# Making the keys of the third mixer inside the stage of the gated recurrence

## The reference, cut to what matters

```python
# rwkv7_branch
a = jax.nn.sigmoid(a0 + pa @ a_up)
g = jax.nn.sigmoid(pg) @ g_up
kk = k * k_k
k = k * (1.0 + (a - 1.0) * k_a)
kk = kk / jnp.maximum(jnp.sqrt(jnp.sum(kk * kk, axis=-1, keepdims=True)), 1e-12)   # per head of 64
y = rwkv7_recurrence(r, decay, k, v, -kk, kk * a)
bonus = jnp.sum(r * k * r_k, axis=-1, keepdims=True) * v
# rglru_branch
xb = causal_dwconv(px, conv_w, conv_b)
gate_a = jax.nn.sigmoid(blockwise(xb, w_ga) + b_ga)
gate_x = jax.nn.sigmoid(blockwise(xb, w_gx) + b_gx)
log_a = LRU_C * gate_a * jax.nn.log_sigmoid(lam)
mult = jnp.sqrt(-jnp.expm1(2.0 * log_a))
u = xb * gate_x * mult
_, h = lax.associative_scan(_lin_combine, (jnp.exp(log_a), u), axis=1)
return h * jax.nn.gelu(py)
```

## Time and profile before

| | |
|---|---|
| median of 3 runs | 2880.39 us (2879.45 to 2884.05) |
| the profiled execution: its time | 2888.27 us |
| its span, first to last instruction | 2886.5 us |
| PE, busy | 2719.0 us, 94% |
| DVE, busy | 1575.4 us, 55% |
| ACT, busy | 1194.2 us, 41% |
| mean granted clock of TensorE | 0.971 |

### The profile page before, as it was taken

How to read it: one execution, slowest core, us unless ns; L and a number is a source line. 1 busy time by engine, 2 the same in 40 slices (tenths; PEclk the granted TensorE clock), 3 DMA queues, 4 the chain that set the end, 5 groups by cost and what they waited for, 6 DMA issues and landing times. The chain is left out here.

```text
span 2886.5 us, 55366 instructions
## 1 busy us (share of the span) xinstructions
PE 2719.0 (94%) x23093; PEld 2125.8 (74%) x23093; DVE 1575.4 (55%) x1950; ACT 1194.2 (41%) x1527; POOL 318.3 (11%) x356
## 2 busy tenths in 40 slices
PE   8999899999999988999999998996779999999998
PEld 6676678888767767777777776843677777788887
DVE  6646454344574655666666665437536544554452
ACT  5544343122454443555555554253215433433232
POOL 5022000000111301001101111022310000000002
PEclk9999999999999998999999999998979999999999
DMA  4200243233220013777777775311004342434231
GB/s 141 67 9 3 59 110 104 79 102 91 89 77 9 3 52 121 264 261 265 268 267 269 271 272 183 95 37 51 7 4 138 88 114 65 121 87 110 73 108 60
DMA packets 351895, 331.31 MB, mean 115 GB/s; under 512 B 17273, under 2 KB 269525, under 8 KB 351605
## 3 DMA queue, kind: packets, MB, share of 16 engines
q1 hardware_dynamic: 348101, 317.76, 35.7%
q0 software_dynamic: 3392, 11.14, 1.1%
q10 hardware_dynamic: 240, 0.07, 0.0%
HBM read 317.41 MB, written 11.53 MB: 114 GB/s over the span
## 5 line engine op out<-in xcount | busy, mean ns | idle before, releaser
L3103 DVE TENSOR_TENSOR experts_w_lo<-experts_raw,experts_w_hi 128x2048 fp32r<-128x2048 f32 (+1 forms) x162 | 335.4, 2079 | 178.1 <-ACT experts_w_hi L3060 169.5
L3060 ACT ACTIVATE experts_w_hi<-experts_raw 128x2048 fp32r<-128x2048 f32 (+1 forms) x162 | 281.8, 1749 | 200.0 <-DMA experts_raw<-in_moe_down 82.1
L3261 PE MATMUL experts_psum<-experts_w_hi,experts_xg_lo 128*128 128x512 f32 x384 | 158.2, 412 | 5.4 <-DVE experts_w_lo L3103 4.1
L1567 PE MATMUL proj_psum<-keep_act_hi,proj_w_lo 128*128 128x512 f32 x360 | 153.4, 426 | 4.4 <-DVE proj_w_lo L1487 4.4
L3263 PE MATMUL experts_psum<-experts_w_hi,experts_xg_hi 128*128 128x512 f32 x384 | 152.5, 397 | 0.0
L3262 PE MATMUL experts_psum<-experts_w_lo,experts_xg_hi 128*128 128x512 f32 x384 | 151.6, 395 | 0.0
L1569 PE MATMUL proj_psum<-keep_act_hi,proj_w_hi 128*128 128x512 f32 x360 | 144.4, 401 | 0.0
L1568 PE MATMUL proj_psum<-keep_act_lo,proj_w_hi 128*128 128x512 f32 x360 | 143.6, 399 | 0.0
L824 PE MATMUL ffn_psum<-keep_act_hi,ffn_w_lo 128*128 128x512 f32 x336 | 133.9, 399 | 1.9 <-DVE ffn_w_lo L686 1.9
L824 PE MATMUL conv_ffn_psum<-keep_act_hi,conv_ffn_w_lo 128*128 128x512 f32 x336 | 133.4, 397 | 1.9 <-DVE conv_ffn_w_lo L686 1.9
L825 PE MATMUL ffn_psum<-keep_act_lo,ffn_w_hi 128*128 128x512 f32 x336 | 133.6, 398 | 0.0
(11 more groups left out here) (895 smaller groups left out, 6698.7 us busy)
## 6 DMA issues: line engine op xcount, KB each, us to landing
experts_raw<-in_moe_gate SPq DMA_DIRECT2D x50, 1024.0 KB, 6.7
experts_raw<-in_moe_up SPq DMA_DIRECT2D x48, 1024.0 KB, 6.9
experts_raw<-in_moe_down SPq DMA_DIRECT2D x64, 768.0 KB, 6.0
conv_ffn_raw<-in_w_ffn_in SPq DMA_DIRECT2D x43, 512.0 KB, 5.0
proj_raw<-in_w_in SPq DMA_DIRECT2D x18, 768.0 KB, 4.4
ffn_raw<-in_ffn_up SPq DMA_DIRECT2D x22, 512.0 KB, 5.2
ffn_raw<-in_ffn_down SPq DMA_DIRECT2D x16, 704.0 KB, 6.5
conv_ffn_raw<-in_w_ffn_out SPq DMA_DIRECT2D x16, 704.0 KB, 5.8
```

The source lines that it names most:

```text
L1567: pe.matmul(out, lo, m.act_hi[:, x, :], start=x == 0, stop=False)
L3060: act.activation(w_hi[v % 2][:, s], raw[ring][:, 0:n], ACT.Copy).then_inc(rounded, 1)
L3103: dve.tensor_tensor(w_lo[v % 2][:, s], raw[(2 * v + q) % RING][:, 0:n], w_hi[v % 2][:, s].bitcast(F32), ALU.subtract).then_inc(split, 1)
L3261: pe.matmul(out, lhs[1][:, first + k, :], w_hi[slot][:, cols], start=begin and k == 0, stop=False)
```

## The change

`rw_keys_phase` is gone. Its steps are now a class `KeysPart`, whose methods are called from the stage of the gated recurrence, renamed `rg_and_keys_phase`, which ends only when the keys, the bonus and seven side tiles (0 to 6) are done. Its sums use the PSUM banks 2 to 5 and the buffer of the bonus instead of a buffer `sq` of their own; the square is taken by DVE instead of ScalarE. The product of `xb` with the gate `gx` now stands ahead of the keys' products on DVE. `kk` and `b` now lie where the norm of the projection stage keeps its squares, and `ld`, `a`, `gx`, `mult` and the gates' weights have other fixed addresses.

```diff
@@ rg_part.scalar
         act.activation(px[:, :, :], mult[:, :, :], ACT.Ln, bias=m.ones[:, 0:1]).then_inc(a_done, 1)
+        keys.logs(act)
+        keep(act, 1)
         act.wait_ge(a_done, 2 * N + 1)
         act.activation(px[:, :, :], px[:, :, :], ACT.Exp, scale=-0.5).then_inc(a_done, 1)
+        keys.roots(act)
         act.activation(mult[:, :, :], mult[:, :, :], ACT.Sqrt, scale=2.0).then_inc(a_done, 1)
-        keep(act, 1)
         keep(act, 2)
@@ the stage, by engine
         def _(sp):
-            for n in range(5):
+            for n in range(6):
                 side.load(sp, n + 2)
                 side.store(sp, n)
+            side.store(sp, 6)
         def _(pe):
             side.tensor(pe, ps, 0, range(7, 8))
-            for n in range(1, 5):
+            keys.sum_squares(pe, rg.steps)
+            for n in range(1, 4):
+                side.tensor(pe, ps, n)
+            keys.sum_products(pe)
+            for n in range(4, 7):
                 side.tensor(pe, ps, n)
         def _(act):
             up.scalar(act)
-            rg.scalar(act, lambda act, n: side.keep(act, ps, n))
+            rg.scalar(act, lambda act, n: side.keep(act, ps, n), keys)
+            side.keep(act, ps, 5)
+            side.keep(act, ps, 6)
         def _(dve):
             rg.start(dve)
             up.vector(dve)
+            keys.squares(dve, up.steps)
+            keys.lengths(dve)
+            rg.scaled(dve)
+            keys.products(dve)
             rg.vector(dve)
+            keys.bonus(dve)
@@ KeysPart
+    def squares(self, dve, kept):
+        m, kk, k = self.m, self.kk, self.k
+        ka = m.params[:, m.columns["k_a"]:m.columns["k_a"] + 4]
+        dve.wait_ge(kept, 8)
+        for j in range(4):
+            self.step(dve, dve.tensor_scalar(kk[:, j, :], k[:, j, :], col(m, "k_k", j), None, ALU.mult))
...
+        self.step(dve, dve.tensor_tensor(self.rows[:, :, :], kk[:, :, :], kk[:, :, :], ALU.mult))
+    def sum_squares(self, pe, free):
+        pe.wait_ge(self.done, self.SQUARES)
+        pe.wait_ge(free, 6)
+        for j in range(4):
+            pe.matmul(self.sums[:, j, :], self.m.pair_ones[:, :], self.rows[:, j, :], start=True, stop=True).then_inc(self.summed, 1)
+    def lengths(self, dve):
+        dve.wait_ge(self.summed, 4)
+        self.step(dve, dve.tensor_scalar(self.rows[:, :, :], self.sums, 1e-24, None, ALU.max))
+    def logs(self, act):
+        act.wait_ge(self.done, self.LENGTHS)
+        act.activation(self.rows[:, :, :], self.rows[:, :, :], ACT.Ln, scale=2.0 ** 30).then_inc(self.rooted, 1)
+    def roots(self, act):
+        act.wait_ge(self.rooted, 1)
+        act.activation(self.rows[:, :, :], self.rows[:, :, :], ACT.Exp, scale=-0.5).then_inc(self.rooted, 1)
+    def products(self, dve):
+        dve.wait_ge(self.rooted, 2)
...
+    def sum_products(self, pe):
+        pe.wait_ge(self.done, self.PRODUCTS)
+        for j in range(4):
+            pe.matmul(self.sums[:, j, :], self.m.pair_ones[:, :], self.rows[:, j, :], start=True, stop=True).then_inc(self.summed, 1)
+    def bonus(self, dve):
+        for j in range(4):
+            dve.wait_ge(self.summed, 4 + j + 1)
+            self.step(dve, dve.tensor_copy(self.rows[:, j, :], self.sums[:, j, :]))
@@ recurrent_part
-            ld_at = start + 2 * 4 * T * 4 + 32 * NCH + TT * 4 * 4 * P * 4
+            kkb = s.sb("kkb", [P, 8, T])
+            kk, b = kkb[:, 0:4], kkb[:, 4:8]
+            ld_at = start + 32 * NCH + TT * 4 * P * 4 * 4
+            row = 4 * T * 4
+            ld, a, gx, mult = (fixed(name, [P, 4, T], ld_at + n * row) for n, name in enumerate(("ld", "a", "rg_gx", "rg_mult")))
-                dense_phase(m, jobs, "proj2", norm_of(m, "norm_mix_g", keep=rstd), slot_size=2 * DT * P)
+                dense_phase(m, jobs, "proj2", norm_of(m, "norm_mix_g", full=kkb, keep=rstd), slot_size=2 * DT * P)
-                rw_keys_phase(m, rw, a, kk, b, bonus, side)
```

More of the change, by code:

```diff
@@ L3369, in rg_part @@
     wa, wx = rg_w
-    xb, ga, gx, mult = (ph.sb(n, [P, N, T]) for n in ("xb", "ga", "gx", "mult"))
+    xb, ga = (ph.sb(n, [P, N, T]) for n in ("xb", "ga"))
     lam, neg = ph.sb("lam", [P, N]), ph.sb("neg", [P, N])
@@ L3449, in start, with gated @@
         dve.tensor_scalar(lam[:, :], neg[:, :], -1.0, None, ALU.mult).then_inc(lam_v, 1)
+    def gated(dve):
+        dve.wait_ge(conv, 4 * N)
+        dve.wait_ge(sig, 2 * N)
+        dve.tensor_tensor(xb[:, :, :], xb[:, :, :], gx[:, :, :], ALU.mult).then_inc(v_done, 1)
     def vector(dve):
-        n = 0
+        n = 1
         def step(ins):
@@ L3473, in vector @@
             step(dve.tensor_tensor(lo[:, j, :], xb[:, j, :], hi[:, j, :].bitcast(F32), ALU.subtract))
-    return Part(sync=sync, tensor=tensor, scalar=scalar, start=start, vector=vector)
+    return Part(sync=sync, tensor=tensor, scalar=scalar, start=start, vector=vector, scaled=gated, steps=sig)
 def shift_beside(m, ph, rw, job, at):
@@ L3511, in shift_beside, with rg_and_keys_phase @@
     return Part(tensor=lambda pe, j, g, f: None, scalar=scalar, vector=vector, gpsimd=lambda pool: None)
-def rg_and_lora_phase(m, px, py, hi, lo, rw, side, lora, ld, a, g, rg_w):
+def rg_and_keys_phase(m, px, py, hi, lo, rw, side, lora, ld, a, g, rg_w, gx, mult, kk, b, bonus):
     with Phase(m, "rg") as ph:
@@ L3518, in rg_and_lora_phase @@
         up = lora_part(m, ph, ps, rw, ld, a, g, lora)
-        rg = rg_part(m, ph, ps, px, py, hi, lo, rg_w, up.steps)
+        rg = rg_part(m, ph, ps, px, py, hi, lo, rg_w, gx, mult, up.steps)
+        keys = KeysPart(m, ph, ps, rw, a, kk, b, bonus)
         block = ph.enter_context(m.nc.Block())
@@ L3533, in _ @@
             side.weigh(pool)
-            for n in range(5):
+            for n in range(7):
                 side.scale(pool, n)
@@ L3608, in lora_part @@
     return Part(tensor=tensor, scalar=scalar, vector=vector, steps=kept)
[L3611 to L3689, removed]
@@ L3951, in recurrent_part @@
             lora = LoraWeights(m, LORA_AT)
+            r = Rule()
+            r.heads, r.decayed = 8, False
+            kkb = s.sb("kkb", [P, 8, T])
+            kk, b = kkb[:, 0:4], kkb[:, 4:8]
             start = -(-m.nc.sbuf_base // 32) * 32
-            ld_at = start + 2 * 4 * T * 4 + 32 * NCH + TT * 4 * 4 * P * 4
+            ld_at = start + 32 * NCH + TT * 4 * P * 4 * 4
             fixed = lambda name, shape, at: m.nc.alloc_sbuf_tensor_at(m.name(name), shape, F32, offset=at)
-            ld, a = fixed("ld", [P, 4, T], ld_at), fixed("a", [P, 4, T], ld_at + 4 * T * 4)
-            rg_w = [fixed(f"rg_w{q}", [P, 4, HD], ld_at + 8 * T * 4 + q * 4 * HD * 4) for q in range(2)]
-            assert rg_w[0] is not None and ld_at + 8 * T * 4 + 8 * HD * 4 <= LORA_AT
+            row = 4 * T * 4
+            ld, a, gx, mult = (fixed(name, [P, 4, T], ld_at + n * row) for n, name in enumerate(("ld", "a", "rg_gx", "rg_mult")))
+            assert ld_at + 4 * row <= LORA_AT
+            rg_w = [fixed(f"rg_w{q}", [P, 4, HD], LORA_AT + 4 * 4 * P * 2 + q * 4 * HD * 4) for q in range(2)]
             with Phase(m, "pxy") as s2:
@@ L3965, in jobs @@
                     return [rows, x, y], shift_beside(m, ph, rw, rows, SIDE_AT)
-                dense_phase(m, jobs, "proj2", norm_of(m, "norm_mix_g", keep=rstd), slot_size=2 * DT * P)
-                rg_and_lora_phase(m, px, py, m.act_hi[:, 4:8], m.act_lo[:, 4:8], rw, side, lora, ld, a, g, rg_w)
-            r = Rule()
-            r.heads, r.decayed = 8, False
-            kk, b = (s.sb(n, [P, 4, T]) for n in ("kk", "b"))
+                dense_phase(m, jobs, "proj2", norm_of(m, "norm_mix_g", full=kkb, keep=rstd), slot_size=2 * DT * P)
+                rg_and_keys_phase(m, px, py, m.act_hi[:, 4:8], m.act_lo[:, 4:8], rw, side, lora, ld, a, g, rg_w, gx, mult, kk, b, bonus)
             r.last = s.sb("last", [P, 4, NCH])
```

39 lines of the change are left out of this document (34 added, 5 removed).

## The result

| | before | the change |
|---|---|---|
| median | 2880.39 us (2878.23 to 2884.05, 5 runs) | 2866.02 us (2860.56 to 2870.4, 5 runs) |
| ratio | | 0.9947, 95% interval 0.9936 to 0.9959 |
| profiled execution: span | 2886.5 us | 2864.8 us |
| mean granted clock | 0.971 | 0.975 |

The change is faster by 14.4 us by the medians, 0.5%; forecast were 19.5 us and 2860.9 us. Timed again beside the kernel before, in two more comparisons, it gave 0.9937 (0.9916 to 0.9957) and 0.9930 (0.9908 to 0.9952), which is 18 and 20 us.

The account below looks back on a forecast made before the run. The keys' stage was taken as a chain with no engine full, costing 35.06 us; merging removes that and adds 15.5, saving 19.5 us, so the 2880.39 us median becomes 2860.9 us, range 2855 to 2868.

Parts of the forecast that it names:

- What bounds the stage: Keys' stage: a chain, no engine full, costing its whole 35.06 us; the merged stage was to end on TensorE's tile passes.
- DVE's first part and ScalarE: Merged stage: squares done at 1931.7, hidden with 2.9 us to spare; ScalarE never waits, keys' Exp done at 1952.4.
- The collision of +0.9: Four key products on DVE: GpSimd's scaling of tile 2 falls in their middle and adds 0.9 us.
- The wait of 2.6 us: TensorE after tile 3: waits from 1958.6 until the key products are ready, 1961.15, before the second sums.
- The clock, 1.0: TensorE over the wait before the second sums: a possible fall to 1.2 GHz costs 0 to 2.3 us, taken as 1.0.
- The end of the stage: Merged stage: ends behind TensorE's last tile at 1989.2 in place of 1973.67, +15.5 of 35.06 us removed.
- Behind the stage: Stages after the merged one: stand as they were, so the 19.5 us saved is carried over.
- the one of the places: Keys, b, gx, mult at new addresses: some 20 DVE operations cost 0.9 us more each, 2879 us; chance 0.03.
- Rival 1 (queues): Side tiles 5 and 6: late DVE makes copy 3 and store 3 hold them, about 2863.6 us; chance 0.14.
- the forecast's 0.4: Tile 5 on TensorE: needs tile 3's copy, 1971.1 against 1971.5, so only 0.4 us to spare.
- Rivals 2 and 4: 2: PE stays at 1.2 GHz, 2909 us, chance 0.01. 4: no clock fall or collision, 2857.3 us, chance 0.12.

## Why the prediction was right, by its steps

It was right in sign and mechanism, and its 2860.9 us was 5.1 below the measured 2866.02. The 19.5 us lie above what the first comparison allows (12 to 18 us by its interval) and within the other two (12 to 24 and 14 to 27).

*What bounds the stage.* Right, and shown: with TensorE's wait removed in three ways (sums moved, wait filled, squares added) A shrank by 2.04, 1.71 and 1.70 us (with the squares the whole stage by 1.35). All three leave DVE's last part alone, so DVE was not the end; with tile 6 taken out it became the end.

*DVE's first part and ScalarE.* Right to a few tenths. The change reached the stage about 3.7 us earlier than the trace of before (side tile 0's last step at 1930.10 in place of 1933.77), so 3.67 is to be taken off the forecast's times. Squares done at 1927.96 (forecast 1931.7, less 3.67: 1928.0), the clamp's start at 1934.77 (1934.6), the keys' Exp done at 1948.5 (1948.7), products ready at 1957.21 (1957.4).

*The collision of +0.9.* Right: 0.89, shown by leaving GpSimd's work out. It fell on the first of the four products and not in their middle. The Trainium skill (GPSIMD Engine Reference, Specifications) says that VectorE's instructions with two SBUF inputs contend with GpSimd, and the 0.89 us agree with it. The collision cost more than its own 0.9, for it also decided on the clock.

*The wait of 2.6 us.* It was 2.00. Of the 0.6 us, 0.2 is the end of tile 3's last pass, which the forecast left out here and the trace counts as busy (three tiles end at 1955.26, the forecast's 1954.9 without it). TensorE was 0.1 to 0.2 later and DVE 0.2 earlier than worked out.

*The clock, 1.0.* This is the term that was mis-sized. I took 1.0 from between 0 and 2.3; the fall came in all three traces of the change and cost 1.7 to 1.8. That is 0.7 to 0.8 us too little. My reason for putting it at the edge was wrong too: I asked how long an idle time must be, 2.4 to 3.4 us by the rows of before. It fell over 2.00 us. The price in the rows of before was misread as well: 15.36 us for 32 passes stands against 13.90 for 32 with the end of the last, not against 13.7, so that fall cost 1.5 and not 1.7.

*The end of the stage.* Forecast 1989.2, less 3.67: 1985.5. It was 1986.05, 0.6 later: 0.8 for the clock, less 0.2 for DVE. By stages the saving was 19.23 in place of 19.5. From side tile 0's last step, which leaves out what varies ahead of it, the time to the first scan of `rw_scale_and_turn_phase` was 74.96 us before and 55.95, 55.95 and 55.94 in the change's three traces: 19.0 us.

*Behind the stage.* I said that the stages there stand as they were. From the first scan to the chunks' product it was 25.47 us before and 25.88, 26.24 and 26.23 in the change's three traces, so 0.4 to 0.8 us went back. The traces show where. The stage ends with TensorE's turns, and these run at 1.2 GHz for longer than before. The us in which the clock came back, first before, then in the first and the second trace of the change (length, TensorE's busy time, granted clock, DMA share, GB/s):

```profile
2029.00:2030.00 1.00, 1.00 (x7) 0.57 0.00 0
```

```profile
2008.00:2009.00 1.00, 1.00 (x7) 0.55 0.08 16
2008.00:2009.00 1.00, 1.00 (x8) 0.62 0.00 0
```

That is about 21.1, 22.9 and 23.7 us after the first scan, and the last four turns begin at 23.12, 23.48 and 23.90. Why the slow stretch ends later was not tested.

*From the trace to the medians.* Stage and what was given back make about 18.5 us; the medians gave 14.4, 18.5 and 21.6, and the ratios 15, 18 and 20 us. In the two profiled executions the spans differ by 21.7 us: 3.45 of it had arisen before the stage began, in code that the change does not touch. The stage began between 1889.58 and 1900.49 us in thirteen traces of programs that are the same up to there but for the places of some buffers. That spread of 11 us is larger than the 4 us between first comparison and trace, so it can hide them, though no run shows that it did; which operation ahead of the stage makes it was not looked for, and stays open. Of the rivals, the one of the places is excluded for the two stages. Rival 1 (queues) did not bind in the change: the copy of tile 3 ended at 1967.11 and tile 5 began at about 1969.4, 2.2 us to spare. Nor was it the slow passes alone that kept it off: with the wait filled, TensorE still had some 0.5 us to spare (copy ended 1968.84, tile 5 at about 1969.4), which is the forecast's 0.4. It bound, with 1.70 us, when the sums moved behind tile 4. Rivals 2 and 4 did not come.

## What to carry to other kernels

A stage in which no engine is full and that ends with a barrier costs its whole length, here 35.06 us for at most 25.71 of work on one engine; put its chain into the idle time of a neighbour, and cost the new end from the engine that has most work there, wait by wait. When a small delay on one engine makes TensorE wait, count the clock as well: here a collision of 0.9 us became 2.6. Before adding filler to keep TensorE busy, change the order, so that useful passes stand where the wait was (2.04 us gained here, against 1.71 with filler), and look at once for the next wait behind it (here the copy of the tile before).

## What the runs showed that I had not expected

The clock can fall after an idle time that is already over: it did in all three traces with a wait of 2.00 us before these sums, when work had begun again. It did not over waits of 1.11, 0.66 and 0.24 us there, nor over those of 1.42 us before the first sums and of 1.70 us before a side tile. And one length does not decide it: the wait of 2.79 us ahead of the next stage's turns stands in nine traces, and the 16 turns behind it took 1.94 us, at full clock, in three of them (the first trace of the change is one, above) and 2.49 to 3.51 us in six. TensorE's timeline in the change's second trace:

```profile
1985.06 3.51 PE L3785 MATMUL rw_scale_psum<-keep_ident,mix_rw 128*128 128x128 f32 x16 [2.79 <-PEq L67]
```

The cost varies too: behind the same wait of 3.33 us, 32 passes took 15.36 us in the kernel before and 16.87 in the one with the new places alone, where 13.90 is full speed. The row of the latter:

```profile
1940.68 16.87 PE L3350 MATMUL rg_psum<-side_h,side_w 128*128 128x512 f32 x32 [3.33 <-ACT side_out L3358]
```

So from a wait of 2 to 3 us a reader of this kernel can give a range for the cost of a fall (1.5 to 3.0 us) and a chance, not a yes or no.

4.65 us of additional work made the stage 1.35 us shorter, because it parted one wait into two.
